# GpSimd finishes two pieces of the last norm in place of VectorE

## What is computed

```python
x = layer_norm(DEEPNORM_ALPHA * x + attn_out, ln1_g[l], ln1_b[l])
hdn = jnp.square(jax.nn.relu(jnp.einsum('bsd,df->bsf', x, w_ff1[l])))
ff_out = jnp.einsum('bsf,fd->bsd', hdn, w_ff2[l])
x = layer_norm(DEEPNORM_ALPHA * x + ff_out, ln2_g[l], ln2_b[l])

def layer_norm(x, g, b):
    mu = jnp.mean(xf, axis=-1, keepdims=True)
    var = jnp.mean(jnp.square(xf - mu), axis=-1, keepdims=True)
    y = (xf - mu) * lax.rsqrt(var + LN_EPS) * g + b
```

## Time and profile before

| | |
|---|---|
| time, median of 3 executions | 1090.94 us (1090.88 to 1091.56) |
| the profiled execution's own time | 1090.75 us |
| its span | 1088.7 us |
| TensorE matmul busy | 1083.9 us (100% of the span) |
| VectorE busy | 808.7 us (74%), 890 instructions |
| ScalarE busy | 571.8 us (53%), 723 instructions |
| GpSimd busy | 21.9 us (2%), 43 instructions |
| granted TensorE clock, mean | 1.0 of full speed |

### The profile page before, as it was taken

One profiled execution on the slowest core, in us unless ns is written; L12 is line 12 of the kernel. 1 busy time (PEld: TensorE's weight loads), 2 busy tenths in 40 slices (PEclk: granted clock), 3 DMA queues, 4 the chain that ended last, 5 costly groups with the idle time before them and its releaser, 6 DMA issues.

```text
span 1088.7 us, 13914 instructions
## 1 busy us (share of the span) xinstructions
PE 1083.9 (100%) x5611; PEld 921.8 (85%) x5611; DVE 808.7 (74%) x890; ACT 571.8 (53%) x723; POOL 21.9 (2%) x43
## 2 busy tenths in 40 slices
PE   9999999999999999999999999999999999999998
PEld 8888888888888888888888888888888888888886
DVE  6587757666656685676699898666776678889998
ACT  6586757565554524445465454344454455554561
POOL 1000000010000000000000000000000000000000
PEclk9999999999999999999999999999999999999999
DMA  9857655657545835665656557466656655655862
GB/s 296 274 182 224 184 182 152 182 172 246 173 155 177 282 101 165 189 189 176 228 176 232 194 194 243 155 188 190 190 175 207 217 175 194 230 195 191 288 215 78
DMA packets 108047, 213.83 MB, mean 196 GB/s; under 512 B 6784, under 2 KB 38016, under 8 KB 107472
## 3 DMA queue, kind: packets, MB, share of 16 engines
q1 hardware_dynamic: 107216, 209.61, 59.6%
q0 software_dynamic: 624, 3.21, 1.0%
q10 hardware_dynamic: 144, 0.13, 0.0%
HBM read 210.83 MB, written 2.10 MB: 196 GB/s over the span
## 4 chain that ended last, share of the span: by engine, by line
PE 98%; DVE 1%; DMA 0%; issue 0%; ACT 0%; DVEq 0%
PE low_ps L791 11%; PE low_ps L628 10%; PE high_ps L791 9%; PE high_ps L812 8%; PE high_ps L811 8%; PE high_ps L813 8%; PE low_ps L522 6%; PE low_ps L526 6%; PE low_ps L524 6%; PE low_ps L797 5%; PE high_ps L797 5%; PE low_ps L633 5%; PE low_ps L812 2%; PE low_ps L811 2%; PE low_ps L813 2%; PE high_ps L569 1%
## 5 line engine op out<-in xcount | busy, mean ns | idle before, releaser
L1297 DVE TENSOR_TENSOR w_lo<-w_raw,w_hi 128x1024 fp32r<-128x1024 f32 x175 | 213.3, 1223 | 126.8 <-ACT w_hi L970 125.7
L970 ACT ACTIVATE w_hi<-w_raw 128x1024 fp32r<-128x1024 f32 x175 | 185.2, 1059 | 184.9 <-PE low_ps L526 66.8
L791 PE MATMUL low_ps<-x1T,w_hi 128*128 128x512 f32 x512 | 177.3, 393 | 0.0
L791 PE MATMUL high_ps<-x1T,w_hi 128*128 128x512 f32 x448 | 155.0, 393 | 0.0
L628 PE MATMUL low_ps<-xT,w_hi 128*128 128x512 f32 x448 | 144.6, 398 | 0.0
L797 PE MATMUL low_ps<-x1T,w_lo 128*128 128x256 f32 x512 | 139.3, 278 | 0.0
L1621 DVE TENSOR_TENSOR w_lo<-w_raw,w_hi 128x1024 fp32r<-128x1024 f32 x72 | 87.1, 1223 | 64.5 <-ACT w_hi L1169 64.5
L1169 ACT ACTIVATE w_hi<-w_raw 128x1024 fp32r<-128x1024 f32 x72 | 76.1, 1059 | 88.7 <-PE low_ps L791 43.4
L797 PE MATMUL high_ps<-x1T,w_lo 128*128 128x256 f32 x448 | 122.1, 278 | 0.0
L813 PE MATMUL high_ps<-w_hi,hid 128*128 128x512 f32 x290 | 112.4, 388 | 0.0
L812 PE MATMUL high_ps<-w_lo,hid 128*128 128x512 f32 x290 | 112.4, 388 | 0.0
(11 more groups left out here) (216 smaller groups left out, 1904.7 us busy)
## 6 DMA issues: line engine op xcount, KB each, us to landing
w_raw<-in_w_ff SPq DMA_DIRECT2D x208, 512.0 KB, 4.4
w_raw<-in_w_in SPq DMA_DIRECT2D x93, 512.0 KB, 4.3
more_raw<-in_w_ff SPq DMA_DIRECT2D x42, 512.0 KB, 5.3
w_raw<-in_w_out SPq DMA_DIRECT2D x32, 512.0 KB, 3.8
x_raw<-in_x_turned SPq DMA_DIRECT2D x8, 256.0 KB, 5.8
y<-in_x SPq DMA_DIRECT2D x8, 256.0 KB, 4.7
side_raw<-in_w_ff SPq DMA_DIRECT2D x4, 512.0 KB, 6.7
w_raw<-in_w_in SPq DMA_DIRECT2D x6, 256.0 KB, 4.7
```

What stands on the lines that cost most here:

```text
L791: return pe.matmul(banks[:, b, :], w_hi[:, slot, cols], x1T[:, t, :, :].rearrange("p h t -> p (h t)"), start=(t == 0 and not lows_open), s ...
L970: act.activation(w_hi[:, slot, :], w_raw[:, slot, :], ACT.Copy).then_inc(w_rounded, units)
L1297: dve.tensor_tensor(w_lo[:, slot, :], w_raw[:, slot, :], w_hi[:, slot, :].bitcast(F32), ALU.subtract).then_inc(w_split, units)
```

## The change

GpSimd takes over the second step of the norm for pieces 1 and 7. It does it in two instructions, a multiplication by 1/std and an addition of the bias, with a semaphore between them (`y2_by_pool`). SP's stores of the two pieces wait for a new semaphore, `y2_finished`; `STORE_ORDER` stays. VectorE's `finish_norm` for piece 1 and `finish_piece(7, 5)` are taken out. `norm_scale` is called for one tile at a time, so that piece 1 lies between the two powers of the last norm on GpSimd.

```diff
+BY_POOL = [1, 7]
...
             if i in COPIED:
                 sp.wait_ge(y2_copied, COPIED.index(i) + 1)
+            elif i in BY_POOL:
+                sp.wait_ge(y2_finished, BY_POOL.index(i) + 1)
             else:
-                sp.wait_ge(y2_ready, i + 1 - len([n for n in COPIED if n < i]))
+                sp.wait_ge(y2_ready, i + 1 - len([n for n in COPIED + BY_POOL if n < i]))
...
         finish_norm(1, count + 1, 0, front[0], y1, ln2_gb, y2_ready)
-        finish_norm(1, count + 2, 0, front[1], y1, ln2_gb, y2_ready)
         add_last(0)
...
         centre(1, 1, LAST_PIECES[7][1], y1, ln2_gb)
-        finish_piece(7, 5)
         centre(1, 1, slice(512, 1024), y1, ln2_gb)
...
-        norm_scale(0)
-
-        norm_scale(1)
+        for tt in range(TT):
+            norm_scale(0, tt)
+
+        def finish_by_pool(n, count, tt, cols):
+
+            pool.wait_ge(gb2_loaded, 32)
+            pool.wait_ge(centred, len(PIECES) + count)
+            pool.wait_ge(std_ready, TT + tt + 1)
+            pool.tensor_scalar(y1[:, tt, cols], y1[:, tt, cols], inv_std[:, tt:tt + 1], None,
+                               ALU.mult).then_inc(y2_by_pool, 1)
+            pool.wait_ge(y2_by_pool, n + 1)
+            pool.tensor_tensor(y1[:, tt, cols], y1[:, tt, cols], ln2_gb[:, 1, cols],
+                               ALU.add).then_inc(y2_finished, 1)
+
+        norm_scale(1, 0)
+        finish_by_pool(0, 2, 0, LAST_PIECES[1][1])
+        norm_scale(1, 1)
+        finish_by_pool(1, 5, 1, LAST_PIECES[7][1])
```

More of the change, by code:

```diff
@@ L312, in hybrid_layer @@
     y2_stats, y2_ready, stored = sem("y2_stats"), sem("y2_ready"), sem("stored")
+    y2_by_pool, y2_finished = sem("y2_by_pool"), sem("y2_finished")
     diag_ready, y2_scaled, y2_copied = sem("diag_ready"), sem("y2_scaled"), sem("y2_copied")
@@ L1866, in rms_scale, with norm_scale @@
             pool.tensor_tensor(o_scale, root, inv_sums[h % 3][:, 0:4:2], ALU.mult).then_inc(scale_ready, 1)
[L1868 to L1878, removed]
+        def norm_scale(norm, tt):
+            n = TT * norm + tt + 1
+            if norm == 0:
+                pool.wait_ge(moments, n)
+                pool.tensor_scalar(var_eps[:, tt:tt + 1], mean_var[:, 2 * tt + 1:2 * tt + 2], EPS,
+                                   None, ALU.add).then_inc(var_ready, 1)
+            pool.wait_ge(var_ready, n)
+            pool.tensor_tensor(inv_std[:, tt:tt + 1], var_eps[:, tt:tt + 1],
+                               minus_half[:, tt:tt + 1], ALU.pow).then_inc(std_ready, 1)
         pool.wait_ge(w_used, SLOTS + 1)
```

## The result

The changed kernel takes 1093.32 us (median of 12 runs, 1093.06 to 1093.92), the kernel before 1091.07 in the same runs. The ratio is 1.0021, 95% interval 1.0013 to 1.0028: slower by 2.25 us, and just over the 0.2% that I had set as the bound of "same" (the interval lies on both sides of it). The forecast was 1092.2, with a range to 1093.3, which the measured time passes by 0.02. The profiled executions say the same: 1093.07 us, span 1091.0, against 1090.75 and 1088.7.

A forecast was written before the change was run, and what follows sets the result against it. TensorE fills 98% of the span, but VectorE's finishing operations bound the tail, feeding SP's and ScalarE's last stores. SP's last landing +1.24 took the profiled 1090.75 to 1092.0; 0.19 for the median gave 1092.2, range 1090.9 to 1093.3 us.

The forecast's parts named there:

- What bounds the tail, and the two paths: Last 9 us: VectorE's finishing operations feed SP's and ScalarE's last stores, landing within 0.16 us; ScalarE's could go 0.55 sooner.
- Piece 1: On VectorE and GpSimd: of 0.66 us removed, 0.15 kept, TensorE's last product deciding; piece 0's finishing held 0.43; no cost.
- The size of GpSimd's operations: GpSimd's 512-column multiplication and addition: 0.86 us each, 1.72 for the pair.
- X + Y - 0.48: Change in the last landing after SP's queue, from GpSimd's two durations X and Y; forecast +1.24 us.
- Rival 4: GpSimd slow per column: with turns, loss passes 2.2 us where X + Y exceeds 2.7; 1094.9 at 2.2 each; chance 0.10.
- The turns: GpSimd and VectorE alternate whole instructions on SBUF: piece 7's multiplication waits until 1083.16, then holds the fourth centre until 1084.02.
- rival 3: GpSimd gets in only when VectorE's queue runs dry, multiplication from 1083.82: +1.9 us, 1092.8; chance 0.12.
- four centres 0.66 apart: Sign on VectorE in the tail: centres at this spacing would mean turns are wrong and rival 1 holds.
- rival 1: No taking of turns that matters: GpSimd's wide operations run without either engine waiting; +0.1 us, 1091.0; chance 0.20.
- The sum: Piece 7 ready on GpSimd at 1085.54, four further SP issues 0.40 apart, landing 2.4 later at 1089.57: +1.24 us.
- The queue's order as the price: In SP's store queue, the late store of piece 7 stands in front of four others.
- The range: Whole kernel, 1090.9 to 1093.3 us: rival 1's 1091.0 less 0.1, to rival 3's 1092.8 plus half a microsecond.

The follow-up runs named there:

- e4: Changed kernel, but GpSimd begins piece 7 only after VectorE has finished piece 8; 1094.77 us, ratio 1.0033 to the kernel before.
- e5: Changed kernel plus six 512-column two-tensor additions on VectorE behind piece 8's finishing; 1093.60 us, one run.
- e6: Changed kernel with GpSimd's multiplication by a scalar operand written as one of two tensors; 1093.26 us, ratio 1.0019 to the kernel before.
- e1: Changed kernel with SP storing piece 7 last; 1091.62 us, ratio 1.0004 to the kernel before.
- e8: Changed kernel with ScalarE multiplying piece 7, GpSimd only adding, and SP storing piece 7 last; 1091.70 us, ratio 1.0005 to the kernel before.
- e9: Changed kernel plus three two-tensor additions on VectorE between the fourth centre and piece 8's finishing; 1095.00 us, one run.
- e7: Changed kernel with VectorE's fourth centre waiting for the third to end, a 0.1 us pause; 1093.17 us, ratio 1.0018 to the kernel before.
- e10: Changed kernel with GpSimd finishing piece 1 only, tile 1's columns 512 to 1023 centred before piece 7, SP storing 3 before 7; 1091.53 us, ratio 1.0003 to before.
- e11: Kernel of e10 with fewer stores: SP joins 3 and 4, ScalarE joins 5 and 6; 1090.99 us, ratio 0.9998 to the kernel before the change.

## Why the prediction was wrong

By its own steps:

- **What bounds the tail, and the two paths**: right. ScalarE's path gained 0.39 (0.55 said), since its last two copies now start at 1084.60 and 1085.03, and SP's set the end.
- **Piece 1**: right that the gain stops at TensorE's last product and that the powers are not disturbed. The additions behind it gained 0.24, not 0.15: the allowance for the signal was too large. That VectorE's finishing of piece 0 would be held 0.43 was wrong: GpSimd's addition was issued after it, at 1077.50, and waited itself (2.13 for 1.26).
- **The size of GpSimd's operations**: this is the step that failed. I took 0.86 for each, 1.72 for the pair, from VectorE's slope. Alone they take 1.58 and 1.26, 2.84. The multiplication was the worse. My estimates by the figures of the Trainium skill (GPSIMD Engine Reference, 3.1) were 1.1 to 1.2 for the addition, close to the 1.26 measured, and 0.5 to 0.8 for the multiplication, at most half of the 1.58 that e4 shows. The forecast's own formula, X + Y - 0.48, gives +2.36 with these two; the loss is 2.25. That they lie so close is partly luck, as the next point shows. Rival 4's point was X + Y over 2.7, and this was passed: the case with the right sizes had a chance of 0.10, because I read the small additions' 0.20 as a sign of a fast engine, though 2 columns say nothing of the cost per column.
- **The turns**: right for two-tensor operations (e5, e6), wrong for the multiplication as written. It got no turn at the change forecast for 1083.16 (it came near 1083.08), got in at 1083.75 ahead of the finishing of piece 8, and held VectorE for 0.23, not 0.86. That is where rival 3 put it (1083.82, chance 0.12), and so the outcome is rival 3's place with rival 4's sizes. My own sign, four centres 0.66 apart, was to show that rival 1 holds; the centres did stand so, but rival 1 is out too, since the multiplication took 2.52 here and 1.58 alone. Rival 3 leaves the same mark. All GpSimd operations whose waits I had read the earlier trace rows were two-tensor ones. The addition then found VectorE idle and did not wait 0.62. Getting in 0.59 later than forecast and not waiting 0.62 nearly cancel.
- **The sum**: the multiplication took 2.52 from 1082.68 against 1.40 from 1082.62, +1.18 at its end; the addition 1.26 against 1.48, -0.22; small gaps +0.05; so piece 7 is ready at 1086.55, not 1085.54. SP's four further issues took 1.83 in place of 1.60, +0.23; the last landing 2.2 in place of 2.4, -0.2. Together 1.0 more than the 1.24 forecast.
- **The queue's order as the price**: right, and shown by e1: 1.8 of the loss goes with one line.
- **The range**: it ended at 1093.3 because it left rival 4 out; half a microsecond "for an addition dearer than 0.86" did not cover a multiplication dearer by 0.7 and an addition dearer by 0.4.

## What to carry to other kernels

Before work goes to an idle engine, ask what stands behind its result in the queue that consumes it: a piece that comes 3 us later cost 2.3 us ahead of four other stores and 0.4 in last place. An engine's operations on one or two columns do not tell its cost per column; here 512 columns took 1.9 and 2.4 times VectorE's 0.66, and where no wide row exists, the range has to take in such a factor. And an operation moved from VectorE to GpSimd, in a stretch where VectorE works on two SBUF tensors, did not run beside it here: it waited for VectorE, or VectorE for it. Piece 1, where only GpSimd waited and had the time for it, cost nothing, but brought no gain either that the times can show.

## What the runs showed of the hardware

- GpSimd multiplies 128x512 float32 by a per-partition scalar in 1.58 us and adds two such tensors in 1.26: the form with fewer inputs is the dearer. The same multiplication written with two tensors ended 0.99 after its turn began (e6).
- The two forms take turns with VectorE in different ways. In these traces the two-tensor form got in at the next change of VectorE's operation, queue or no queue, and held an operation with two SBUF tensors for 0.78 to 1.06 (e5, e6, e8). The scalar form was passed over at one change between such operations (2.52 in all) and at four (4.33, e9); it got in at a pause of a tenth of a microsecond (e7) and, without a pause, when VectorE's next operation read one SBUF tensor (piece 1). It held VectorE for 0.23 to 0.35. Why it got in ahead of the last operation in e9 is not settled.
- Stores issued back to back on SP slow down: 0.38 for the first step, then 0.47, 0.48 and 0.50 in the changed kernel, where the weight loads of the earlier trace rows stood 0.40 apart. The last store of 256 KB landed 2.2 after its issue in the changed kernel, and 2.6 to 2.8 after it in e8, e10 and e11.
